# Experts on blocks of 96 places, with tokens held in the array in groups of 32 and four column groups of 256 weight columns

## The chip, the cores and the metric

The kernel runs on one core of a Trainium2 chip. The metric is device microseconds of one execution, taken as the median of several runs. Tensors are float32 throughout.

## What is computed

The program runs two hybrid transformer layers and then a third one of another kind; the change touches only the mixture of experts that ends the third. There are 1024 tokens of width 1024 (`D`), 32 experts in 4 groups of 8, and each token goes to the best two experts of its best group:

```python
logit_g = (h @ w_rg + b_rg).astype(F32)
grp = jnp.argmax(logit_g, axis=-1)
...
top_v, top_i = lax.top_k(logit_e, TOP_K)                    # TOP_K = 2
gate = jax.nn.softmax(top_v, axis=-1) * p_grp
expert = (grp[:, None] * EXPERTS_PER_GROUP + top_i).reshape(-1)
...
def expert_block(args):
    xb, e = args
    g, u = jnp.split(xb @ w_up[e], 2, axis=-1)              # w_up[e]: 1024 x 1024
    return (jax.nn.silu(g) * u) @ w_down[e]                 # w_down[e]: 512 x 1024
...
y = y[dest] * gate.reshape(-1)[order][:, None].astype(h.dtype)
return jax.ops.segment_sum(y, tok_sorted, num_segments=n_tok)
```

The 2048 pairs of token and expert are sorted by expert and padded to whole blocks of places, so that each block has one expert. The reference uses 128 places a block, but its result doesn't depend on that number. The reference's own routing, worked out on its inputs, gives the 32 experts between 43 and 87 tokens each, 2048 in all.

## The kernel before

Two functions matter. `mix_dispatch` (stage `disp`) scores the tokens, counts them per expert, and builds three tables: `rows` (which row of `XN` each place of each block takes), `gates` (the weight of each place) and `table` (the expert of each block, and the numbers of pairs of blocks). Its long chain of small VectorE steps ends at line 3245. While that runs, SyncE already loads the weights of the first block.

`block_experts` (stage `bexp`, lines 3384 to 3576) then runs over the blocks, two per turn of a hardware loop whose count is read from `table`; `i` is the turn and `j` the buffer, 0 or 1. Each engine has its own program with the same loop:

- SyncE loads the weights of block `n + 2` into the buffers of block `n`: the gate half and the up half of `w_up` (2 MB each, L3437, in rows of 2 KB), and `w_down` (2 MB in rows of 4 KB, L3439). Its order is gate, up, down for `j = 0`, then for `j = 1`. It waits for the last product that reads each buffer (`gate_done`, `up_done`, `downed`).
- TensorE, in `body`: eight products of 512 columns into `gu[0]` (the gate, L3537), the four transposes of the last block's middle values (`hid_turn`, L3515), eight products into `gu[1]` (the up half), eight transposes of the next block's tokens (`turn`, L3509), and the last block's second product (`down`, L3525, two halves of four products of 512 columns into `acc`). The tokens (`xT`, 128 by 128) are stationary, and the weights stream. So the order is up(n), down(n-1), up(n+1), down(n).
- ScalarE takes the exponential of the gate (L3492), copies the transposed middle values out of PSUM (`take`, L3480) and writes the result times the gate weight (`write`, L3486, two of 512 columns).
- VectorE finishes the silu and multiplies by the up half (L3564 to L3572), and then scales and shifts the next block's transposed tokens into `xT` (`modulate`, L3557).
- GpSimd multiplies by the layer's output gate (L3451), adds the block's rows to `F` with an indirect DMA (L3458), and gathers the rows of a block four further on with another (L3447).

After the last block, `gather_norm` reads `F`, normalises it and stores the result.

An fp32 product is two MATMUL records in the trace, each with its weight load (LDWEIGHTS, engine PEld); a transpose is one. The kernel already has one place where tokens in a group of 32 are held stationary and four column groups of 256 weight columns follow one another: the context part of `down` in the first layer's experts, line 2043 (stage `l0exp`).

Of the kernel before, what the change touches and what calls it, by code (L numbers as in the profile page):

```python
# [3042 lines left out]
MAX_BLOCKS = (SEQ * TOP + N_EXP * 127) // 128  # L3043
# [3 lines left out]
def mix_dispatch(nc, name, GO, wt, gt, X, cols_a, cols_b, w_group, b_group, w_expert, b_expert, consts, XN, F, rows, gates, table, w_up, w_down,  # L3047
# [6 lines left out]
    with Stage(nc, name) as st:  # L3054
# [10 lines left out]
        row_of = cst[:, 336:336 + T]  # L3065
        spare = cst[:, 336 + T:337 + T]
        places = cst[:, 337 + T:337 + T + 128]
# [27 lines left out]
        in_place = sb("in_place", [128, TOP * T, 128])  # L3095
# [9 lines left out]
        slot_sum = acc[1][:, 0:2 * MAX_BLOCKS]  # L3105
# [5 lines left out]
        steps, exps, counted, tabled = sem("steps"), sem("exps"), sem("counted"), sem("tabled")  # L3111
        marks = {}
        with nc.Block(no_gpsimd_drain=True) as block:
            @block.vector
            def _(ve):
# [81 lines left out]
                for q in range(1, SEQ // 128):  # L3197
                    step(V_.scalar_tensor_tensor(nb[:, :], cnt[:, 0:N_EXP], float(128 * q), nb[:, :], ALU.is_gt, ALU.add))
# [8 lines left out]
                step(V_.tensor_scalar(pstart[:, :], pstart[:, :], 128.0, None, ALU.mult))  # L3207
# [5 lines left out]
                step(V_.tensor_scalar(inside[:, :], flat, 1.0 / 128, 1.0, ALU.mult, ALU.subtract))  # L3213
# [3 lines left out]
                step(V_.scalar_tensor_tensor(at_place[:, :], inside[:, :], -128.0, flat, ALU.mult, ALU.add))  # L3217
# [3 lines left out]
                for half in range(2):  # L3221
                    part = slice(half * each, (half + 1) * each)
                    step(V_.tensor_tensor(in_place[:, part, :], places.unsqueeze(1).broadcast_to([128, each, 128]),
                                          at_place[:, part].unsqueeze(2).broadcast_to([128, each, 128]), ALU.is_equal))
# [10 lines left out]
                step(V_.tensor_scalar(rows[:, :], slot_sum[:, 0:MAX_BLOCKS], spare, None, ALU.add))  # L3235
                marks["rows"] = count[0]
                step(V_.tensor_copy(gates[:, :], slot_sum[:, MAX_BLOCKS:2 * MAX_BLOCKS]))
# [10 lines left out]
            def _(sp):  # L3248
# [23 lines left out]
                for h in range(2):  # L3272
                    sp.dma_start(first_w[h], w_up[bass.ds(e, 1), :, h * FF:(h + 1) * FF].rearrange("e (k p) n -> p (e k) n", p=128)).then_inc(first_in[h], 16)
                sp.dma_start(first_w[2], w_down[bass.ds(e, 1), :, :].rearrange("e (k p) n -> p (e k) n", p=128)).then_inc(first_in[2], 16)
# [3 lines left out]
            @block.gpsimd  # L3278
            def _(po):
                nc.gpsimd.memset(eps[:, :], EPS).then_inc(eps_made, 1)  # L3280
                for j in range(NX):
                    po.wait_ge(stored[j], START + 16 * (T // NX))
                po.wait_ge(steps, START + marks["rows"])
                for j in range(2):
                    po.indirect_dma_start(first_x[j], None, XN, bass.IndirectOffsetOnAxis(ap=rows[:, j:j + 1], axis=0)).then_inc(x_in[j], 16)

            @block.scalar
            def _(act):
# [32 lines left out]
                nc.scalar.activation(e1[:, :], e1[:, :], ACT.Exp).then_inc(exps, 1)  # L3321

# [61 lines left out]
def block_experts(nc, name, XN, rows, gates, F, out_gate, table, cols_a, cols_b, w_up, w_down, first_w, first_in, first_x, x_in, identity):  # L3384

    B = 2
    with Stage(nc, name, LOOPED) as st:
        sb, ps, sem = st.sb, st.ps, st.sem
        wu = [first_w[0:2], [sb(f"wu1{h}", [128, KD, FF]) for h in range(2)]]
        wd = [first_w[2], sb("wd1", [128, KF, D])]  # L3390
        og = sb("og", [128, D])
        idx = [sb(f"idx{j}", [128, 1], i32) for j in range(B)]
        out_idx = [sb(f"out_idx{j}", [128, 1], i32) for j in range(B)]
        xg = first_x
        xT = [sb(f"xT{j}", [128, KD, 128]) for j in range(B)]
        ex = sb("ex", [128, FF])
        hidR = [sb(f"hidR{j}", [128, FF]) for j in range(B)]
        hid = [sb(f"hid{j}", [128, KF, 128]) for j in range(B)]
        y = [sb(f"y{j}", [128, D]) for j in range(B)]
        turnedP = ps("turned", [128, KD, 128])  # L3400
        gu = [ps(f"gu{h}", [128, FF]) for h in range(2)]
        hidP = ps("hidP", [128, KF, 128])
        acc = [ps(f"acc{c}", [128, 512]) for c in range(2)]
        gate_in, up_in, down_in = ([st.adopt(first_in[i]), sem(f"{n}1")] for i, n in enumerate(("gate_in", "up_in", "down_in")))
        turned, x_ready, gate_done, up_done, hid_turned, hid_taken, downed, y_ready, freed, raised, steps = (
            [sem(f"{n}{j}") for j in range(B)] for n in ("turned", "x_ready", "gate_done", "up_done", "hid_turned", "hid_taken",
# [4 lines left out]
        passed_ve, passed_po, passed_act = sem("passed_ve"), sem("passed_po"), sem("passed_act")  # L3411

        def turns(eng, body):
            rest = eng.value_load(table[0:1, MAX_BLOCKS + 1:MAX_BLOCKS + 2], min_val=1, max_val=MAX_BLOCKS // 2 - 1)
            body(0, 0, True, False)
            with eng.Fori(0, rest) as i:
                body(i, 1, False, False)
                body(i + 1, 0, False, False)
            body(rest, 1, False, True)
            return rest  # L3420

        with nc.Block(no_gpsimd_drain=True) as block:
# [19 lines left out]
            def _(po):  # L3442
                def gather(i, j):
                    wait_alone(po, turned[j], LOOPED + i, passed_po)
                    nc.gpsimd.tensor_copy(idx[j][:, :], rows[:, bass.ds(i * B + j, 1)]).then_inc(idx_made[j], 1)
# [3 lines left out]
                def add_out(i, j, first):  # L3449
                    wait_alone(po, y_ready[j], LOOPED + i * 2 + 2, passed_po)  # L3450
# [4 lines left out]
                    nc.gpsimd.tensor_copy(out_idx[j][:, :], rows[:, bass.ds(i * B + j, 1)]).then_inc(out_made[j], 1)  # L3455
# [20 lines left out]
            def _(act):  # L3476
                def take(i, j):
                    act.wait_ge(hid_turned[j], LOOPED + i + 1)
                    act.wait_ge(downed[j], LOOPED + i * 2)
                    nc.scalar.activation(hid[j][:, :, :], hidP[:, :, :], ACT.Copy).then_inc(hid_taken[j], 1)  # L3480

                def write(i, j):
                    for c in range(2):
                        act.wait_ge(downed[j], LOOPED + i * 2 + c + 1)
                        wait_alone(act, freed[j], LOOPED + i, passed_act)
                        nc.scalar.activation(y[j][:, c * 512:(c + 1) * 512], acc[c][:, :], ACT.Copy, scale=gates[:, bass.ds(i * B + j, 1)]).then_inc(y_ready[j], 1)  # L3486

                def body(i, j, first, last):
                    act.wait_ge(gate_done[j], LOOPED + i + 1)
                    if not first:  # L3490
                        act.wait_ge(steps[1 - j], LOOPED + (i + j) * 4)
# [352 lines left out]
```

## Time and profile before

| | before |
|---|---|
| median of 3 runs | 4724.09 us (4721.94 to 4727.69) |
| the profiled execution, its span | 4732.4 us |
| instructions | 59744 |
| TensorE busy (matmul) | 4229.9 us (89%) |
| VectorE busy | 2033.2 us (43%) |
| ScalarE busy | 1069.4 us (23%) |
| GpSimd busy | 738.1 us (16%) |
| DMA traffic | 769.59 MB, mean 163 GB/s |
| weights of the last experts (L3437) | 64 issues of 2 MB, median 16.0 and 16.7 us to landing |

The profile is of one execution; its own time is the span of 4732.4 us, which is 8.3 us (0.18%) above the median of the runs, and no time around it is recorded. Busy shares are means over the whole program; a change in one stage is read from that stage. The stage of the last experts reaches from about 3979 us to 4704 us.

### The profile page before, as it was taken

What the parts mean: (1) busy time and instruction counts of PE and PEld (TensorE: products, weight loads), DVE (VectorE), ACT (ScalarE), POOL (GpSimd) and SP (SyncE); (2) the same over time, 40 slices, a digit from 0 to 9 for tenths busy, and PEclk for the clock granted to TensorE, in tenths of its full rate; (3) what the DMA queues carried; (4) which work ended last, traced back from release to release, by engine and by line L of the source; (5) the groups of instructions that cost most, each with busy time, mean ns of one, the idle gap of its engine ahead of it and who ended that gap; (6) DMA issues with size and microseconds to landing.
All of it is one profiled execution on the core that took longest, in us unless ns stands there. A gap on an engine that the chain in (4) does not pass through costs nothing. (4 is left out here: it accounts for less than half of the span.)

```text
span 4732.4 us, 59744 instructions
## 1 busy us (share of the span) xinstructions
PE 4229.9 (89%) x22975; PEld 2790.0 (59%) x22975; DVE 2033.2 (43%) x3879; ACT 1069.4 (23%) x2077; POOL 738.1 (16%) x851
## 2 busy tenths in 40 slices
PE   6998999977999798999968997999788896999996
PEld 4664556445888565566436885776566454444443
DVE  1223556135555322556254452111686666333332
ACT  1112346030000110335130001110564421111111
POOL 0110000301111011000301100000550330222221
PEclk8998999988999899999978998999899897999998
DMA  7115110367887411401169995111532115999997
GB/s 252 36 47 125 23 42 7 129 254 273 274 267 252 138 62 57 108 1 48 44 250 326 338 327 168 49 37 42 144 86 87 59 40 209 316 334 339 334 334 244
DMA packets 366851, 769.59 MB, mean 163 GB/s; under 512 B 59716, under 2 KB 136172, under 8 KB 365384
## 3 DMA queue, kind: packets, MB, share of 16 engines
q1 hardware_dynamic: 337032, 653.92, 40.2%
q0 software_dynamic: 23856, 90.19, 7.4%
q10 hardware_dynamic: 5712, 22.02, 1.2%
q8 instruction: 172, 2.82, 0.2%
q14 instruction: 79, 0.65, 0.0%
HBM read 650.62 MB, written 115.45 MB: 162 GB/s over the span
## 5 line engine op out<-in xcount | busy, mean ns | idle before, releaser
L3537 PE MATMUL bexp_gu<-X,bexp_xT 128*128 128x512 f32 x512 | 227.6, 598 | 3.0 <-DVE bexp_xT L3557 3.0
L3537 PE MATMUL bexp_gu<-bexp_wu,bexp_xT 128*128 128x512 f32 x512 | 225.1, 592 | 3.1 <-DVE bexp_xT L3557 3.1
L625 PE MATMUL p_ring<-p_hT,p_wc 128*128 128x256 f32 x1008 | 220.4, 381 | 4.8 <-DMA p_wc<-in_w_in 4.8
L625 PEld LDWEIGHTS p_ring<-p_hT,p_wc 128*128 128x128 f32 x1008 | 192.3, 191 | 31.6 <-issue 5.2
L3564 DVE TENSOR_SCALAR bexp_ex<-bexp_ex 128x512 f32<-128x512 f32 x32 | 15.1, 471 | 368.7 <-ACT bexp_ex L3492 368.7
L633 PE MATMUL p_ring<-p_wt,p_hT 128*128 128x400 f32 (+2 forms) x480 | 170.8, 516 | 0.0
L3537 PEld LDWEIGHTS bexp_gu<-X,bexp_xT 128*128 128x128 f32 x512 | 97.0, 192 | 119.8 <-issue 116.5
L3537 PEld LDWEIGHTS bexp_gu<-bexp_wu,bexp_xT 128*128 128x128 f32 x512 | 95.9, 190 | 117.7 <-issue 117.7
L1117 PE MATMUL l0mla_scores<-l0mla_kT,l0mla_qT 96*128 96x512 f32 (+1 forms) x312 | 142.9, 546 | 21.1 <-DMA l0mla_qT<-RT 15.3
L2026 PE MATMUL l0exp_gu<-l0exp_xT,l0exp_wg 128*128 128x160 f32 x1024 | 155.0, 305 | 4.5 <-DVE l0exp_xT L2070 4.5
L2026 PE MATMUL l0exp_gu<-l0exp_xT,l0exp_wu 128*128 128x160 f32 x1024 | 151.1, 301 | 1.5 <-DMA l0exp_wu<-in_exp_w_up 1.5
L2026 PEld LDWEIGHTS l0exp_gu<-l0exp_xT,l0exp_wg 128*128 128x128 f32 x1024 | 143.7, 192 | 11.4 <-issue 6.2
L3451 POOL TENSOR_TENSOR bexp_y<-bexp_y,bexp_og 128x1024 f32<-128x1024 f32 x32 | 75.0, 2344 | 481.6 <-ACT bexp_y L3486 481.6
L2043 PE MATMUL l0exp_acc<-l0exp_wd,l0exp_hid 128*32 128x256 f32 (+1 forms) x768 | 144.1, 455 | 2.6 <-DVE l0exp_hid L2085 2.6
L2026 PEld LDWEIGHTS l0exp_gu<-l0exp_xT,l0exp_wu 128*128 128x128 f32 x1024 | 144.0, 192 | 1.9 <-DMA l0exp_wu<-in_exp_w_up 1.9
L1117 PE MATMUL l1mla_scores<-l1mla_kT,l1mla_qT 96*128 96x512 f32 (+1 forms) x288 | 133.8, 551 | 12.3 <-DMA l1mla_qT<-RT 12.3
L3486 ACT ACTIVATE bexp_y<-bexp_acc,slot_gates 128x512 f32<-128x512 f32 x64 | 44.0, 687 | 419.6 <-PE bexp_acc L3525 419.6
L633 PEld LDWEIGHTS p_ring<-p_wt,p_hT 128*128 128x128 f32 x480 | 91.1, 190 | 76.1 <-issue 38.3
L2026 PE MATMUL l1exp_gu<-l1exp_xT,l1exp_wg 128*128 128x128 f32 x1024 | 127.4, 279 | 3.0 <-DMA l1exp_wg<-in_exp_w_gate 3.0
L2026 PEld LDWEIGHTS l1exp_gu<-l1exp_xT,l1exp_wg 128*128 128x128 f32 x1024 | 123.2, 195 | 10.6 <-issue 7.2
L2026 PE MATMUL l1exp_gu<-l1exp_xT,l1exp_wu 128*128 128x128 f32 x1024 | 125.7, 276 | 3.0 <-DMA l1exp_wu<-in_exp_w_up 3.0
L633 PE MATMUL l0proj_ring<-l0proj_wt,l0proj_hT 128*128 128x464 f32 x320 | 126.2, 552 | 0.0
(683 smaller groups left out, 8392.9 us busy)
## 6 DMA issues: line engine op xcount, KB each, us to landing
X<-in_w_expert_up SPq DMA_DIRECT2D x32, 2048.0 KB, 16.0
bexp_wu<-in_w_expert_up SPq DMA_DIRECT2D x32, 2048.0 KB, 16.7
l0exp_wg<-in_exp_w_gate SPq DMA_DIRECT2D x16, 2048.0 KB, 9.3
l0exp_wu<-in_exp_w_up SPq DMA_DIRECT2D x16, 2048.0 KB
l0exp_wd<-in_exp_w_down SPq DMA_DIRECT2D x16, 2048.0 KB, 12.6
l1exp_wg<-in_exp_w_gate SPq DMA_DIRECT2D x16, 2048.0 KB, 9.5
l1exp_wu<-in_exp_w_up SPq DMA_DIRECT2D x16, 2048.0 KB
l1exp_wd<-in_exp_w_down SPq DMA_DIRECT2D x16, 2048.0 KB, 13.1
```

What stands on the lines that cost most here:

```text
L625: mm = nc.tensor.matmul(out[:, i * PC:(i + 1) * PC], wc[:, k, b * 128:(b + 1) * 128], hT[ch % 2][:, k, :], start=(k == 0), stop=(k == KD - 1))
L633: mm = nc.tensor.matmul(out[:, at_out:at_out + n], hT[ch % 2][:, k, t * 128:(t + 1) * 128], wt[:, k, s:s + n], start=(k == 0), stop=(k == ...
L1117: mm = nc.tensor.matmul(scores[u % NBUF][:, at:at + n], qT[p % 2][a][:, row:row + 128], k[:, r:r + n], start=True, stop=True)
L2026: mm = nc.tensor.matmul(gu[g % 2][:, h, :], w[j][:, k, f * 128:(f + 1) * 128], xT[j][:, k, :], start=(k == 0), stop=(k == KD - 1))
L2043: mm = nc.tensor.matmul(acc[g % 3][cap * q:cap * (q + 1), 0:n_y], hid[j][:, f, at[s]:at[s] + cap], wd[j][:, f, at_y:at_y + n_y], start=(f ...
L3451: nc.gpsimd.tensor_tensor(y[j][:, :], y[j][:, :], og[:, :], ALU.mult).then_inc(weighed[j], 1)
L3486: nc.scalar.activation(y[j][:, c * 512:(c + 1) * 512], acc[c][:, :], ACT.Copy, scale=gates[:, bass.ds(i * B + j, 1)]).then_inc(y_ready[j], 1)
L3537: mm = nc.tensor.matmul(gu[h][:, :], xT[j][:, k, :], wu[j][h][:, k, :], start=(k == 0), stop=(k == KD - 1))
L3564: nc.vector.tensor_scalar(ex[:, :], ex[:, :], 1.0, None, ALU.add).then_inc(steps[j], 1)
```

## The change

A block has 96 places instead of 128, in three groups (`r`) of 32. In `block_experts` the stationary operand is now a group of 32 tokens, and four products (`c` = 0 to 3) with a quarter of the weight columns each go to the four column groups of the array, and so to the four 32-partition groups of PSUM. The up product of a group holds 128 gate columns and the matching 128 up columns in one bank, so that gate and up are no longer two phases; the three groups are. The middle values lie with their quarter `c` on a partition group, so three transposes of 128 by 128 give the stationary operands of `down`. `w_up` of a block is one load of 4 MB with rows of 4 KB. The result is written by ScalarE in twelve pieces of 32 by 256. In `mix_dispatch` the tables are made for 96 places; ScalarE makes the copies of the gate weights on four partition groups. The loop of ScalarE, VectorE and TensorE opens with a wait for SyncE (`opened`). The core of the diff:

```diff
-MAX_BLOCKS = (SEQ * TOP + N_EXP * 127) // 128
+BLOCK = 96
+GROUPS = BLOCK // 32
+MAX_BLOCKS = (SEQ * TOP + N_EXP * (BLOCK - 1)) // BLOCK
 MAX_BLOCKS += MAX_BLOCKS % 2
...
-                for q in range(1, SEQ // 128):
-                    step(V_.scalar_tensor_tensor(nb[:, :], cnt[:, 0:N_EXP], float(128 * q), nb[:, :], ALU.is_gt, ALU.add))
+                for q in range(1, -(-SEQ // BLOCK)):
+                    step(V_.scalar_tensor_tensor(nb[:, :], cnt[:, 0:N_EXP], float(BLOCK * q), nb[:, :], ALU.is_gt, ALU.add))
...
-                step(V_.tensor_copy(gates[:, :], slot_sum[:, MAX_BLOCKS:2 * MAX_BLOCKS]))
...
+                act.wait_ge(steps, START + marks["rows"])
+                for c in range(4):
+                    for r in range(GROUPS):
+                        nc.scalar.activation(gates[32 * c:32 * c + 32, r, :], slot_sum[32 * r:32 * r + 32, MAX_BLOCKS:2 * MAX_BLOCKS], ACT.Copy).then_inc(gated4, 1)
+                act.wait_ge(gated4, START + 4 * GROUPS)
...
+    R = GROUPS
+    COLS = 4
+    HN = FF // COLS
+    YN = D // COLS
...
-        gu = [ps(f"gu{h}", [128, FF]) for h in range(2)]
-        acc = [ps(f"acc{c}", [128, 512]) for c in range(2)]
+        gu = [ps(f"gu{r}", [128, 512]) for r in range(R)]
+        acc = ps("acc", [128, 2, 2, YN])
...
         def turns(eng, body):
+            eng.wait_ge(opened, 1)
...
-                        for h, (done, landed) in enumerate(((gate_done, gate_in), (up_done, up_in))):
-                            sp.wait_ge(done[j], LOOPED + i)
-                            sp.dma_start(wu[j][h][:, :, :], w_up[bass.ds(e, 1), :, h * FF:(h + 1) * FF].rearrange("e (k p) n -> p (e k) n", p=128)).then_inc(landed[j], 16)
-                        sp.wait_ge(downed[j], LOOPED + i * 2)
+                        sp.wait_ge(up_done[j], LOOPED + i * R)
+                        sp.dma_start(wu[j][:, :, :], w_up[bass.ds(e, 1), :, :].rearrange("e (k p) n -> p (e k) n", p=128)).then_inc(up_in[j], 16)
+                        sp.wait_ge(downed[j], LOOPED + i * R)
...
                 def write(i, j):
-                    for c in range(2):
-                        act.wait_ge(downed[j], LOOPED + i * 2 + c + 1)
-                        wait_alone(act, freed[j], LOOPED + i, passed_act)
-                        nc.scalar.activation(y[j][:, c * 512:(c + 1) * 512], acc[c][:, :], ACT.Copy, scale=gates[:, bass.ds(i * B + j, 1)]).then_inc(y_ready[j], 1)
+                    wait_alone(act, freed[j], LOOPED + i, passed_act)
+                    for r in range(R):
+                        if r != 0:
+                            act.wait_ge(downed[j], LOOPED + i * R + r + 1)
+                        if r == 0:
+                            act.wait_ge(downed[j], LOOPED + i * R + min(R, 2))
+                        for c in range(COLS):
+                            rows_c = slice(32 * c, 32 * c + 32)
+                            nc.scalar.activation(y[j][32 * r:32 * r + 32, c * YN:(c + 1) * YN], acc[rows_c, r // 2, r % 2, :], ACT.Copy,
+                                                 scale=gates[rows_c, r, bass.ds(i * B + j, 1)]).then_inc(y_ready[j], 1)
...
-                    for c in range(2):
+                    for r in range(R):
                         for f in range(KF):
-                            mm = nc.tensor.matmul(acc[c][:, :], hid[j][:, f, :], wd[j][:, f, c * 512:(c + 1) * 512], start=(f == 0), stop=(f == KF - 1))
+                            for c in range(COLS):
+                                mm = nc.tensor.matmul(acc[32 * c:32 * c + 32, r // 2, r % 2, :], hid[j][:, r, 32 * f:32 * f + 32],
+                                                      wd[j][:, f, c * YN:(c + 1) * YN], start=(f == 0), stop=(f == KF - 1))
                         mm.then_inc(downed[j], 1)
...
-                    for h in range(2):
-                        pe.wait_ge((gate_in, up_in)[h][j], LOOPED + (i + 1) * 16)
+                    pe.wait_ge(up_in[j], LOOPED + (i + 1) * 16)
+                    for r in range(R):
+                        if not first:
+                            pe.wait_ge(steps[1 - j], LOOPED + (i + j) * 4 * R - 4 * (R - 1 - r))
                         for k in range(KD):
-                            mm = nc.tensor.matmul(gu[h][:, :], xT[j][:, k, :], wu[j][h][:, k, :], start=(k == 0), stop=(k == KD - 1))
-                        mm.then_inc((gate_done, up_done)[h][j], 1)
-                        if h == 0 and not first:
+                            both = wu[j][:, k, :].rearrange("p (h c n) -> p h c n", h=2, c=COLS)
+                            for c in range(COLS):
+                                mm = nc.tensor.matmul(gu[r][32 * c:32 * c + 32, 0:2 * HN].rearrange("p (h n) -> p h n", h=2), xT[j][:, k, 32 * r:32 * r + 32],
+                                                      both[:, :, c, :], start=(k == 0), stop=(k == KD - 1))
+                        mm.then_inc(up_done[j], 1)
+                        if r == 0 and not first:
                             hid_turn(i + j - 1, 1 - j)
```

VectorE's four silu steps run three times on 128 by 128 instead of once on 128 by 512. GpSimd's gather and its indirect add handle 96 rows a block, and its multiplication waits for all twelve pieces.

## Rows read from the trace of the kernel before

**Rows 1.** The page's second part, DMA share in tenths, 40 equal slices.
```profile
DMA  7115110367887411401169995111532115999997
```

**Rows 2.** Busy time by stretch: PE, PEld, DVE, ACT, POOL, granted clock, DMA share, GB/s.
```profile
4050.00:4200.00 150.00, 150.00 (x413) 70.85 (x412) 54.85 (x84) 16.49 (x28) 37.03 (x35) 1.00 0.98 335
```

**Rows 3.** Timeline of TensorE over one block: start, length, engine, line, tile, records.
```profile
4115.06 7.03 PE L3537 MATMUL bexp_gu<-X,bexp_xT 128*128 128x512 f32 x16
4121.92 0.60 PE L3515 MATMUL bexp_hidP<-identity,bexp_hidR 128*128 128x128 f32 x4
4122.36 7.03 PE L3537 MATMUL bexp_gu<-X,bexp_xT 128*128 128x512 f32 x16
4129.23 1.04 PE L3509 MATMUL bexp_turned<-identity,X 128*128 128x128 f32 x8
4130.10 7.03 PE L3525 MATMUL bexp_acc<-bexp_wd,bexp_hid 128*128 128x512 f32 x16
4136.97 7.03 PE L3537 MATMUL bexp_gu<-bexp_wu,bexp_xT 128*128 128x512 f32 x16
```

**Rows 4.** Timeline of SyncE over the same block: the issues of weight loads.
```profile
4115.39 0.37 SPq L3439 DMA_DIRECT2D YA<-in_w_expert_down  x1
4116.59 3.14 SPq L3437 DMA_DIRECT2D bexp_wu<-in_w_expert_up  x2
4137.30 0.37 SPq L3439 DMA_DIRECT2D bexp_wd<-in_w_expert_down  x1
```

**Rows 5.** DMA queues, 4050 to 4650 us: packets, MB, share of 16 engines.
```profile
q1 hardware_dynamic: 71214, 172.52, 80.2%
q0 software_dynamic: 7776, 28.32, 17.7%
```

**Rows 6.** Busy time by stretch, for the DMA share and GB/s that end each row.
```profile
4115.30:4118.00 2.70, 2.70 (x7) 1.14 (x6) 0.00 (x0) 0.69 (x1) 1.74 (x1) 1.00 0.61 124
4124.80:4130.20 5.40, 5.40 (x20) 2.82 (x19) 3.33 (x3) 0.00 (x0) 0.00 (x0) 1.00 1.04 297
4131.00:4137.00 6.00, 6.00 (x16) 2.65 (x15) 2.17 (x7) 0.69 (x1) 0.00 (x0) 1.00 1.04 391
11.50:31.50 20.00, 11.12 (x120) 4.30 (x124) 0.00 (x0) 1.69 (x5) 0.22 (x1) 0.91 1.03 423
```

**Rows 7.** Line 2043: timeline of TensorE, its last 32 records as a stretch, weight loads.
```profile
1506.65 8.89 PE L2043 MATMUL l0exp_acc<-l0exp_wd,l0exp_hid 128*128 128x512 f32 x48
1515.48 2.44 PE L2026 MATMUL l0exp_gu<-l0exp_xT,l0exp_wg 128*128 128x160 f32 x16
...
1513.60:1515.35 1.75, 1.75 (x33) 0.94 (x32) 1.00 0.97 359
...
L2043 PEld LDWEIGHTS l0exp_acc<-l0exp_wd,l0exp_hid 128*32 128x32 f32 x512 | 15.0, 109 | 20.4 <-issue 12.1
```

**Rows 8.** Timeline of TensorE: a long run of records on column groups of 32.
```profile
3803.34 2.22 PE L2704 MATMUL gs_bank<-gs_v,gs_kbT 128*32 128x64 f32 x144
3805.48 0.70 PE L2649 MATMUL gs_acc<-out_wt,NT 128*128 128x512 f32 x1
```

**Rows 9.** Groups by line and form: busy us and mean ns.
```profile
L2081 DVE RECIPROCAL l1exp_ex<-l1exp_ex 128x128 f32<-128x128 f32 x64 | 61.0, 954 | 2.2
L2380 ACT ACTIVATE da_probT<-da_turned 128x256 f32<-128x256 f32 x32 | 12.0, 375 | 3.3 <-PE da_turned L2326 3.3
L3557 DVE TENSOR_SCALAR bexp_xT<-bexp_turned,cols 128x128 f32<-128x128 f32 x256 | 84.5, 402 | 9.5 <-PE bexp_turned L3509 4.7 <-issue 3.0
```

**Rows 10.** The stage's start: timelines of TensorE and SyncE, and a stretch.
```profile
3979.81 1.96 PE L3509 MATMUL bexp_turned<-identity,X 128*128 128x128 f32 x8 [6.21 <-DMA X<-XN,slot_rows]
3980.72 0.34 SPq L3426 DMA_DIRECT2D bexp_og<-gates  x1
4001.20:4005.40 4.20, 1.06 (x10) 0.82 (x8) 3.33 (x9) 0.00 (x0) 1.15 (x2) 1.00 1.04 387
```

**Rows 11.** DMA queues, 2520 to 2870 us, where TensorE's code has no loop.
```profile
q8 instruction: 19, 0.31, 0.4%
```

More of the change, by code:

```diff
@@ L3104, in mix_dispatch @@
         cnt = acc[0][:, 512:1024]
-        slot_sum = acc[1][:, 0:2 * MAX_BLOCKS]
+        slot_sum = acc[1][0:BLOCK, 0:2 * MAX_BLOCKS]
         w_in, eps_made = sem("w_in"), sem("eps_made")
@@ L3405, in block_experts @@
-        turned, x_ready, gate_done, up_done, hid_turned, hid_taken, downed, y_ready, freed, raised, steps = (
-            [sem(f"{n}{j}") for j in range(B)] for n in ("turned", "x_ready", "gate_done", "up_done", "hid_turned", "hid_taken",
+        wu = [first_w[0], sb("wu1", [128, KD, 2 * FF])]
+        wd = [first_w[1], sb("wd1", [128, KF, D])]
+        og = sb("og", [BLOCK, D])
+        idx = [sb(f"idx{j}", [BLOCK, 1], i32) for j in range(B)]
+        out_idx = [sb(f"out_idx{j}", [BLOCK, 1], i32) for j in range(B)]
@@ L3407, in block_experts @@
+        up_in, down_in = ([st.adopt(first_in[i]), sem(f"{n}1")] for i, n in enumerate(("up_in", "down_in")))
+        turned, x_ready, up_done, hid_turned, hid_taken, downed, y_ready, freed, raised, steps = (
+            [sem(f"{n}{j}") for j in range(B)] for n in ("turned", "x_ready", "up_done", "hid_turned", "hid_taken",
                                                          "downed", "y_ready", "freed", "raised", "steps"))
@@ new lines, in body @@
+                def body(i, j, first, last):
+                    for r in range(R):
+                        act.wait_ge(up_done[j], LOOPED + i * R + r + 1)
+                        if not first:
+                            act.wait_ge(steps[1 - j], LOOPED + (i + j) * 4 * R - 4 * (R - 1 - r))
+                        nc.scalar.activation(ex[r][:, :], gu[r][:, 0:HN], ACT.Exp, scale=-1.0).then_inc(raised[j], 1)
+                        if r == 0 and not first:
+                            take(i + j - 1, 1 - j)
@@ L3490, in body @@
                     if not first:
-                        act.wait_ge(steps[1 - j], LOOPED + (i + j) * 4)
-                    nc.scalar.activation(ex[:, :], gu[0][:, :], ACT.Exp, scale=-1.0).then_inc(raised[j], 1)
-                    if not first:
-                        take(i + j - 1, 1 - j)
                         write(i + j - 1, 1 - j)
@@ L3764, in second_block @@
         table = keep("table", [128, MAX_BLOCKS + 3], i32)
-        rows, block_gates = keep("slot_rows", [128, MAX_BLOCKS], i32), keep("slot_gates", [128, MAX_BLOCKS])
+        rows, block_gates = keep("slot_rows", [128, MAX_BLOCKS], i32), keep("slot_gates", [128, GROUPS, MAX_BLOCKS])
         YA = keep("YA", [128, LAT_TILES, A_HEADS * A_DV])
-        first_x = [X[:, j, :] for j in range(2)]
-        half = KD * FF // D
-        first_w = [X[:, CTX_TILES + h * half:CTX_TILES + (h + 1) * half, :].rearrange("p a n -> p (a n)").rearrange("p (k n) -> p k n", n=FF) for h in range(2)]
+        first_x = [X[0:BLOCK, j, :] for j in range(2)]
+        first_w = [X[:, CTX_TILES:CTX_TILES + KD, :]]
         first_w.append(YA[:, :, :].rearrange("p a n -> p (a n)").rearrange("p (k n) -> p k n", n=D))
-        first_in = [nc.alloc_semaphore(f"first_{n}_in") for n in ("gate", "up", "down")]
+        first_in = [nc.alloc_semaphore(f"first_{n}_in") for n in ("up", "down")]
         x_in = [nc.alloc_semaphore(f"first_x_in{j}") for j in range(2)]
```

111 lines of the change are left out of this document (54 added, 57 removed).

## The prediction

> **What bounds the kernel now.** I read the page's 40 slices first: the last experts fill the slices near 9 at the end of the DMA row [rows 1]. Then the busy time of a stretch inside that stage: TensorE is busy 150.00 of 150 us at the full clock (1.00, the 2.4 GHz level), the 16 DMA engines 98%, at 335 GB/s; VectorE, ScalarE and GpSimd 55, 16 and 37 us [rows 2]. So two resources are nearly full, and the question is which binds. The timeline of TensorE answers it: one block is gate 6.87 us (start to start), middle transposes 0.44, up 6.87, token transposes 0.87, down 6.87, and the next block starts at once; 4136.97 − 4115.06 = 21.91 us, with no gap [rows 3]. The timeline of SyncE shows how near the DMA is: all 6 MB of a bunch (down weights of block n, up weights of block n+1) are issued when down(n) ends, 4115.39 to 4116.59, and the next bunch at 4137.30 [rows 4]. A bunch has one block period to arrive. It nearly fills it: 80.2% of 21.91 us is weights (17.6 us), 17.7% gather and indirect add (3.88 us) [rows 5]. Of the period 2.7 us is a start at 124 GB/s, which moves what 391 GB/s moves in 0.86: 1.84 us are lost between issue and full rate [rows 6]. TensorE binds, the DMA follows at under 1 us.
>
> **The change, part by part.** *Number of blocks.* The reference's routing gives an expert at most 87 tokens, under 96, so 32 blocks stay 32, and weight traffic stays 6.29 MB a block.
>
> *TensorE's products.* Before: 24 products of 512 columns, two records each, 6.87/16 = 0.429 us a record, 20.6 us a block [rows 3]. After: up has 3 groups × 8 × 4 products, down 3 × 4 × 4, 144 products, 288 records of 256 columns. One alone should take half of 0.429; what matters is whether four column groups run side by side. Line 2043 has this very form: 128 rows, 32 stationary columns, 256 moving. From its start to the next line's are 8.83 us; 16 records of 512 columns take 6.87, which leaves 1.96 for 32 records, and the stretch of these 32 alone has 1.75 [rows 7]. So four records (a "four") take 1.75/8 = 0.219 us, as long as one: the overlap is full, and 0.21 us goes to entering and leaving the form. A burst of 32 might live off a filled queue; but 144 records on groups of 32 run in 2.14 us, 14.9 ns each, where I need one per 55 ns, so issue doesn't limit a long run [rows 8]. Per block: 72 fours × 0.219 = 15.8; token transposes 0.87; three of four middle transposes 0.33; two runs between transposes at 0.21, 0.42. P = 17.4 us (from 17.0 without the changes of form to 18.9 if each four costs 1.96/8). This moves work off the path: up 10.5 us, down 5.3.
>
> *Other engines, hidden.* VectorE has three chains on 128 columns; the last group's is a reciprocal of 0.95, three steps and an exponential of under 0.4 each, then `modulate`'s eight at 0.33 busy (84.5/256) [rows 9]: about 5.4 us after the up products end, and TensorE first does transposes and down, 0.87 + 5.3 = 6.2. It hides with 0.8 us left; without that cover each further microsecond would be one per block. ScalarE's twelve pieces at about 0.375 [rows 9] are 4.5 us; the first eight start a group before down ends, the rest end 2.5 us after it, ahead of the next exponential, 3.5 us into the next up. Behind them waits GpSimd (all twelve), 2 us later than before; its gather is for a block more than a period away. ScalarE's waits on `downed` queue only that exponential.
>
> *Weights.* The 4 MB load is one piece: up can't start on its first half, so a bunch must land whole by the start of the block two after. SyncE still issues at the end of down; its wait for `up_done` had always passed by then [rows 4]. Transfer time S: 6.29 MB at 391 GB/s (2 KB rows) is 16.1 us, at 423 (4 KB rows, the load of the program's start, no other traffic) 14.9 [rows 6]; all rows are 4 KB now, but gathers run beside: I take 15.7. Gather and add fall by a quarter, 3.88 to 2.9; while they run both together move only 297 GB/s [rows 6]. S = 18.6 (17.8 to 19.0; by the share of busy time, 17.6 + 2.9 = 20.5).
>
> *The sum of a period.* With P = 17.4 TensorE no longer binds. From the end of down(n): 1.84 us of start, S, then up(n+3) may begin, and P later down(n+2) ends: two periods = 1.84 + 18.6 + 17.4 = 37.8, 18.9 each. That is above S and P, so it sets the pace. Gain 21.91 − 18.9 = 3.0 us a block.
>
> *The ends.* At the start stand three more small steps of VectorE's `nb` chain, and the wait for `opened`, behind which TensorE now loads the count: its first transposes, at 3979.81 before, can't come ahead of SyncE's opening, which ends just before its first issue at 3980.72 [rows 10]. For both I take 2 us late (0 to 3, an estimate from these two starts), but block 0's up is 3 us shorter, so block 1 starts where it did. Blocks 1 and 2 gain 4.5 each; block 3 waits 3.0 for the first bunch: −6. Blocks 3 to 30: 28 × 3.0 = −84. The last block and its down gain 6.6 and lose 2.0 to the late pieces: −4.6. Sum −95: from the median 4724 to 4629, and the span from 4732 to about 4638; the profiled execution stands 0.18% above the median, and I carry the difference over.
>
> **A rule and the rows.** The Trainium skill (TensorE: Matmul & The Clock Gate, Part 3: Packing small matmuls — row/col tiling) measured 3.07 times for four row groups and 2.38 for three column groups. By 3.07 a four would take 4 × 0.215/3.07 = 0.28 us, an estimate, and P 21.8: no gain at all. The rows above show 0.219, a factor of 3.9, and I go by them.
>
> **The rivals.** *Weights bind harder.* If the start is lost on every bunch (1.84 + 18.6 = 20.4) or S is the busy share's 20.5, a period is 20.5: 28 × 1.4 = 39, and 8 at the ends: 4677. For it: the share is measured in this very loop. Against: it counts packets as busy while they wait at the start of a bunch, and a bunch issued while another flows has no start. The two don't add: for the kernel before they would make 17.6 + 3.9 + 1.84 = 23.3, more than the 21.91 measured. With a fetch of code on top (next) it could reach 4710.
>
> *Code.* The loop's TensorE code grows from 60 to 299 records a block. No instruction traffic stands in the loop before [rows 5], while straight code fetches 19 packets of 16 KB in 350 us [rows 11]. If each turn must fetch again at its jump, it costs about what a load's start costs, 1.8 to 2.7 us per two blocks [rows 6], partly inside the wait for weights: at most 15 × 2.7 = 40, 4669. The Trainium skill (Runtime: NRT & Kernel Launch, Instruction fetch mechanics) says both that TensorE's code memory has 128 KiB, in which this loop fits, and that only two blocks of 16 KiB are held and a jump out of them stalls; no run here shows which.
>
> *The fours don't hold up.* The up products read their 256 columns in two runs of 128, over 48 fours, which no row shows. The point of no change is 0.282 us a four ((21.9 − 1.6)/72). If one weight load per four were exposed (109 ns each; they now overlap, 15.0 us busy for 512 [rows 7]), a four is 0.33, P = 25.3, and 31 × 3.4 − 5 makes 4824. Idle TensorE could also lose its clock; but after 3.1 idle us of 4.2 it was still 1.00 [rows 10].
>
> *More blocks.* If the chip's routing pushed an expert over 96, the loop would take two more blocks: 4629 + 38 = 4667. Nothing but a rounding at a margin of nine tokens speaks for it.
>
> **How the numbers follow.** Weights and TensorE in turn at 18.2 to 19.8 a block: 0.55, 4607 to 4656. Weights harder or code fetched again, 4660 to 4712: 0.26. Fours slower: 0.10, of which 0.02 near no change. More blocks 0.03. Unnamed stalls 0.06, in thirds to a half. Low end: S 17.8 and P 17.0 give 18.3, 17 less, and 5 at the ends: 4606. The high end reaches to 4700, over most of the harder weights, and leaves out the slow rival and a few more, under 2 in 10. A measurement of this kernel tells 0.2% (9 us) from no change. Faster 0.85 (0.55 + 0.24 + 0.03 + 0.03), same 0.05, slower 0.10.
>
> **What would show it.** In the profile after: fours 0.22 us apart at the new up and down lines; TensorE idle some 1.5 us a block before the first up product, ended by the load of `w_up`; periods alternating near 17.4 to 20.4 or even at S; DMA share 0.98 or more at 370 to 390 GB/s; 32 indirect adds; no instruction queue in the loop. It would be wrong if VectorE's `modulate` ended the wait before up (its 0.8 us gone), if fours stood at 0.28 or more, or if the clock in the stage fell under 1.00.

## The result and the profile after

The median went from 4723.0 to 4697.6 us, a ratio of 0.9936 with a 95% interval of 0.9924 to 0.9949: 25 us faster where the prediction had 95. The profiled execution took 4688.9 us; its span, 4687.0, is 45.4 less than that of before, and 13.5 of these lie in unchanged code ahead of the stage. The first matmul of the count in `mix_dispatch`, before and after (timelines of TensorE):

```profile
3953.00 1.22 PE L3374 MATMUL disp_acc<-disp_both,disp_cst 128*128 128x256 f32 x2 [13.20 <-DVE disp_upto L3186]
...
3939.47 1.22 PE L3380 MATMUL disp_acc<-disp_both,disp_cst 128*128 128x256 f32 x2 [13.21 <-DVE disp_upto L3189]
```

From there to the end are 779.4 us before and 747.5 after, so the stage itself gave 31.9 us, and that is the number to explain. TensorE is no longer busy all the time, and its granted clock is under full, 0.95 (busy time by stretch, columns as in [rows 2]):

```profile
4050.00:4200.00 150.00, 129.00 (x2153) 74.38 (x2149) 62.85 (x146) 53.60 (x124) 37.56 (x36) 0.95 0.93 336
```

Blocks now come in pairs of unlike length. Timeline of TensorE over one pair, columns as in [rows 3]; the bracket is the idle time ahead and what ended it:

```profile
4116.39 5.35 PE L3561 MATMUL bexp_gu<-bexp_wu,bexp_xT 128*32 128x256 f32 x64 [5.16 <-DMA bexp_wu<-in_w_expert_up]
4121.67 0.55 PE L3535 MATMUL bexp_hidP<-identity,bexp_hidR 128*128 128x128 f32 x3
4122.15 7.11 PE L3561 MATMUL bexp_gu<-bexp_wu,bexp_xT 128*32 128x256 f32 x128
4129.19 0.88 PE L3529 MATMUL bexp_turned<-identity,X 96*128 96x96 f32 x8
4130.00 5.39 PE L3546 MATMUL bexp_acc<-YA,bexp_hid 128*32 128x256 f32 x96
4135.21 3.64 PE L3561 MATMUL bexp_gu<-X,bexp_xT 128*32 128x256 f32 x64
4138.78 0.55 PE L3535 MATMUL bexp_hidP<-identity,bexp_hidR 128*128 128x128 f32 x3
...
4158.07 5.06 PE L3561 MATMUL bexp_gu<-bexp_wu,bexp_xT 128*32 128x256 f32 x64 [5.57 <-DMA bexp_wu<-in_w_expert_up]
```

The products are as fast as hoped: 64 records (16 fours) in 4138.78 − 4135.21 = 3.57 us, 0.223 a four; the down product's 24 fours in 5.21 us, 0.217. But from block 3 to block 29 every odd block waits over 5 us for `bexp_wu`. Behind the first of the two waits shown, the first 64 records take 5.28 us instead of 3.57: in that stretch the granted clock is 0.68, between the two levels of 1.2 and 2.4 GHz (0.50 and 1.00), so part of it ran at the lower one. The pair lasts 41.68 us, 18.82 and 22.86. The timeline of SyncE shows when its loads were issued:

```profile
4111.43 0.37 SPq L3451 DMA_DIRECT2D bexp_wd<-in_w_expert_down  x1
4113.00 0.38 SPq L3449 DMA_DIRECT2D X<-in_w_expert_up  x1
4135.59 0.37 SPq L3451 DMA_DIRECT2D YA<-in_w_expert_down  x1
4136.81 0.37 SPq L3449 DMA_DIRECT2D bexp_wu<-in_w_expert_up  x1
4152.69 0.37 SPq L3451 DMA_DIRECT2D bexp_wd<-in_w_expert_down  x1
```

The bunch of 4135.59 (call it A) meets a DMA that has run dry; the bunch of 4152.69 (B) is issued while A still flows. Busy time by stretch, for the last three columns (clock, DMA share, GB/s): the time around A's first issue, A's start, a stretch after it, the time of the bunch B before A, and the slow 64 records:

```profile
4135.20:4136.50 1.30, 1.30 (x28) 0.78 (x24) 0.00 (x0) 1.23 (x4) 0.00 (x0) 1.00 0.00 0
4136.50:4139.20 2.70, 2.70 (x47) 1.48 (x39) 0.00 (x0) 2.57 (x6) 0.00 (x0) 1.00 0.90 247
4139.20:4144.00 4.80, 4.80 (x90) 2.89 (x92) 3.44 (x3) 1.42 (x5) 3.29 (x3) 1.00 1.02 416
...
4116.00:4134.00 18.00, 17.61 (x279) 10.33 (x283) 7.10 (x19) 1.49 (x5) 4.86 (x5) 0.91 1.02 378
4116.40:4121.70 5.30, 5.30 (x65) 2.83 (x65) 0.00 (x0) 0.00 (x0) 3.67 (x5) 0.68 1.03 423
```

Blocks 3 and 31 and the end of the stage, timeline of TensorE and then of ScalarE:

```profile
4032.42 1.93 PE L3561 MATMUL bexp_gu<-bexp_wu,bexp_xT 128*32 128x256 f32 x16 [6.21 <-DMA bexp_wu<-in_w_expert_up]
...
4613.58 5.35 PE L3561 MATMUL bexp_gu<-bexp_wu,bexp_xT 128*32 128x256 f32 x64 [3.48 <-DMA bexp_wu<-in_w_expert_up]
...
4636.59 8.15 PE L3546 MATMUL bexp_acc<-bexp_wd,bexp_hid 128*32 128x256 f32 x96 [4.48 <-ACT bexp_hid L3492]
...
4630.07 5.87 ACT L3503 ACTIVATE bexp_y<-bexp_acc,slot_gates 32x256 f32<-32x256 f32 x12 [3.20 <-PE bexp_acc L3546]
4635.97 0.49 ACT L3492 ACTIVATE bexp_hid<-bexp_hidP 128x384 f32<-128x384 f32 x1
```

The last block's middle tile stands on ScalarE behind the twelve pieces of the block before. TensorE waits 4.48 us for it and then takes 8.15 us for a down product of 5.2.

### The profile page after: what moved, and what is told of

It reads as the page before. It is cut to its first block and busy times, and to the rows that moved or that the text cites. A ratio compares the mean times of both kernels' runs of the same rounds, so it can differ in the third digit from the quotient of the medians.

```text
span 4687.0 us, 76558 instructions
## 1 busy us (share of the span) xinstructions
PE 4100.3 (87%) x30623; PEld 2786.7 (59%) x30623; DVE 2057.6 (44%) x4137; ACT 1213.1 (26%) x2473; POOL 734.7 (16%) x851
## 5 line engine op out<-in xcount | busy, mean ns | idle before, releaser
L3561 PE MATMUL bexp_gu<-bexp_wu,bexp_xT 128*32 128x256 f32 x3072 | 202.9, 428 | 82.9 <-DMA bexp_wu<-in_w_expert_up 78.4
L3503 ACT ACTIVATE bexp_y<-bexp_acc,slot_gates 32x256 f32<-32x256 f32 x384 | 179.1, 466 | 144.4 <-PE bexp_acc L3546 135.6
L625 PEld LDWEIGHTS p_ring<-p_hT,p_wc 128*128 128x128 f32 x1008 | 192.3, 191 | 31.7 <-issue 5.3
L3561 PEld LDWEIGHTS bexp_gu<-bexp_wu,bexp_xT 128*32 128x32 f32 x3072 | 107.3, 123 | 173.2 <-issue 124.9
L3590 DVE TENSOR_SCALAR bexp_ex<-bexp_ex 128x128 f32<-128x128 f32 x96 | 52.4, 546 | 336.0 <-ACT bexp_ex L3511 336.0
L3561 PE MATMUL bexp_gu<-X,bexp_xT 128*32 128x256 f32 x3072 | 174.1, 383 | 2.7 <-DVE bexp_xT L3582 2.7
L3463 POOL TENSOR_TENSOR bexp_y<-bexp_y,bexp_og 96x1024 f32<-96x1024 f32 x32 | 75.7, 2364 | 457.5 <-ACT bexp_y L3503 457.5
L3561 PEld LDWEIGHTS bexp_gu<-X,bexp_xT 128*32 128x32 f32 x3072 | 98.3, 111 | 70.8 <-issue 5.0
L1995 ACT ACTIVATE l0exp_ex<-l0exp_gu 128x160 f32<-128x160 f32 x64 | 19.5, 304 | 444.4 <-PE l0exp_gu L2026 444.4
## 6 DMA issues: line engine op xcount, KB each, us to landing
X<-in_w_expert_up SPq DMA_DIRECT2D x16, 4096.0 KB, 21.9
```

Of the source, the lines that this page charges most:

```text
L625: mm = nc.tensor.matmul(out[:, i * PC:(i + 1) * PC], wc[:, k, b * 128:(b + 1) * 128], hT[ch % 2][:, k, :], start=(k == 0), stop=(k == KD - 1))
L1995: nc.scalar.activation(ex[g % 2][:, :], gu[g % 2][:, 0, :], ACT.Exp, scale=-1.0).then_inc(raised, 1)
L3463: nc.gpsimd.tensor_tensor(y[j][:, :], y[j][:, :], og[:, :], ALU.mult).then_inc(weighed[j], 1)
L3503: nc.scalar.activation(y[j][32 * r:32 * r + 32, c * YN:(c + 1) * YN], acc[rows_c, r // 2, r % 2, :], ACT.Copy, scale=gates[rows_c, r, bass ...
L3561: mm = nc.tensor.matmul(gu[r][32 * c:32 * c + 32, 0:2 * HN].rearrange("p (h n) -> p h n", h=2), xT[j][:, k, 32 * r:32 * r + 32], both[:, : ...
L3590: nc.vector.tensor_scalar(ex[r][:, :], ex[r][:, :], 1.0, None, ALU.add).then_inc(steps[j], 1)
```

## The experiments

The theory after these readings: TensorE's part of the prediction holds, and what was lost is lost because SyncE issues a load late; the DMA then starts from a standstill, TensorE waits, and its clock falls. "Stage" in the table is from block 0's first up product to the end of the span; "a block" is the time from block 8's start to block 30's, by 22. Both are of the profiled execution. The kernels were timed on several occasions, so each median goes with the before beside it.

| kernel | median, us | before beside it | ratio (95%) | stage | a block |
|---|---|---|---|---|---|
| before | 4723.0 | | | 747.7 | 21.91 |
| after | 4697.6 | 4723.0 | 0.9936 (0.9924 to 0.9949) | 715.0 | 20.80 |
| e1_order | 4616.2 | 4726.7 | 0.9764 (0.9748 to 0.9780) | 635.9 | 18.45 |
| e2_warm | 4684.2 | 4726.7 | 0.9909 (0.9892 to 0.9925) | 705.4 | 20.25 |
| e3_eighth | 4590.4 | 4726.7 | 0.9713 (0.9693 to 0.9732) | 603.4 | 17.10 |
| e4_order_before | 4723.9 | 4726.7 | 0.9997 (0.9987 to 1.0006) | 747.8 | 21.91 |
| e5_tail | 4608.2 | 4721.6 | 0.9761 (0.9743 to 0.9779) | 630.1 | 18.51 |
| e6_half_rows | 4583.5 | 4721.6 | 0.9703 (0.9683 to 0.9722) | 601.9 | 17.10 |
| e7_halves | 4625.7 | 4721.6 | 0.9788 (0.9771 to 0.9804) | 643.8 | 18.73 |
| e8_skip | 4607.8 | 4728.8 | 0.9745 (0.9729 to 0.9761) | 626.9 | 18.38 |

**The order of the loads.** In the pair above the up product that reads `bexp_wu` ends at 4129.19, and its next load is issued at 4136.81, because the wait for `downed` of the block before stands in front of it. Each up load moves ahead of that wait. In outline, not in the words of the kernel (the loop's last turn leaves out the load that has no block):

```diff
-    up_done[j]  -> load wu[j] of block n;    downed[j] -> load wd[j] of block n
+    up_done[1]  -> load wu[1] of block 2i+1; downed[0] -> load wd[0] of block 2i
+    up_done[0]  -> load wu[0] of block 2i+2; downed[1] -> load wd[1] of block 2i+1
```

> The changed kernel with one thing moved: SyncE issues the up weights of the next block as soon as up_done frees their buffer, ahead of the down weights that wait for downed. Same bytes, same instructions on TensorE. Theory (the late issue sets the pace): the transfers then run back to back at the 18.0 us that the second bunch of a pair took, so a block takes 18.2 to 18.6 us in place of 20.7 to 20.8, the wait for bexp_wu falls from 5.2 to 6.2 us to under 1 us, the granted clock of 4050 to 4500 us rises from 0.94 to at least 0.98, and 28 blocks give 60 to 70 us: 4628 to 4640 us. Rival (the DMA engines are full: 94% of 20.7 us is 19.5 us of packet time a block, whoever issues them): a block takes 19.5 to 20.7 us, TensorE keeps waiting, 4663 to 4698 us.

Measured: 81 us less than the changed kernel by the medians, 79 in the stage. In its loop the clock and the DMA are at full, and the waits are 1.0 to 1.8 us where under 1 was expected (a stretch; the first and the last block that the table's 18.45 is counted from):

```profile
4050.00:4200.00 150.00, 143.64 (x2504) 84.42 (x2500) 76.71 (x171) 59.05 (x138) 41.22 (x40) 1.00 1.03 380
...
4124.53 1.72 PE L3573 MATMUL bexp_gu<-X,bexp_xT 128*32 128x256 f32 x28 [1.84 <-DMA X<-in_w_expert_up]
...
4530.41 3.66 PE L3573 MATMUL bexp_gu<-X,bexp_xT 128*32 128x256 f32 x64 [1.05 <-DMA X<-in_w_expert_up]
```

The theory stands, and the rival that the DMA engines were full at 94% falls: they moved the same bytes in 18.45 us a block. The gain is above the 60 to 70 expected mainly because blocks 2 to 6 run at TensorE's own 17.10 us, their loads being ahead; only from block 7 on do the transfers bind.

**The same order in the kernel before.** The edit is the same, with its two up loads.

> The kernel before with the same move of SyncE's loads (up weights of the next block ahead of the down weights). Theory (TensorE sets its pace, no wait for weights in its loop): within 0.2% of 4723 us. Rival (the order of the loads is worth something by itself): 20 us or more faster.

Measured 2.8 us less, inside the interval of no change. The order is worth nothing while TensorE takes 21.9 us; it is the change that makes it matter.

**TensorE alone.** The loads in the loop shrink to one tile each, and the rest of the products reads what the buffers held (the same for `wd`):

```diff
-    sp.dma_start(wu[j][:, :, :], w_up[bass.ds(e, 1), :, :] ...)
+    sp.dma_start(wu[j][:, 0:1, :], w_up[bass.ds(e, 1), 0:128, :] ...)
```

> The changed kernel with only the first of the eight (up) and four (down) weight tiles loaded in the loop, 0.5 MB each instead of 4.2 and 2.1 MB; the rest of the products reads what the buffers held, so this part of the computation is left out. Theory (TensorE's own work is what the prediction said, and all beyond it is the loads): no wait for weights, granted clock 1.00, a block takes TensorE's 17.1 to 17.5 us, 28 blocks save 90 to 103 us: 4595 to 4610 us. Rival (something else in the block's chain, GpSimd's gather or ScalarE's twelve pieces, stands close behind): 18.5 us or more a block, 4635 us or more.

```profile
4050.00:4200.00 150.00, 150.00 (x2627) 89.06 (x2623) 83.10 (x176) 61.03 (x143) 43.50 (x42) 1.00 0.44 110
```

17.10 us a block, each one the same, TensorE never idle. Nothing but the loads stands between the changed kernel and TensorE's pace; with the DMA less than half busy, neither ScalarE's pieces nor VectorE nor the gather is next in line.

**The clock by itself.** TensorE's wait is filled with work and the loads are left as they were:

```diff
+    if j == 1 and not last:
+        for _ in range(24):
+            nc.tensor.matmul(hidP[:, 3, :], identity[:, :], identity[:, :], start=True, stop=True)
     pe.wait_ge(up_in[j], LOOPED + (i + 1) * 16)
```

> The changed kernel with 24 matmuls of the identity by itself put on TensorE ahead of its wait for the up weights in every odd body of the loop (some 5 us of work, into a part of hidP that nothing reads): the wait of 5.2 to 6.2 us is filled, the loads are untouched. Theory (the lower granted clock after the wait is a cost of its own): the first 64 matmuls of the up product take 3.6 us again in place of 5.3 to 6.4, and as the end of the block's down product issues the next bunch, what is won goes into the pair's 41.5 us until the other bunch, which has 1.3 us to spare, binds: 1.2 to 2 us a pair, 15 to 28 us in all, 4670 to 4683 us. Rival (the loads alone set the pace, TensorE's speed after the wait is given back at the next wait): within 0.2% of the changed kernel, 4690 to 4705 us.

```profile
4158.62 5.39 PE L3546 MATMUL bexp_acc<-bexp_wd,bexp_hid 128*32 128x256 f32 x96
4163.94 5.62 PE L3556 MATMUL bexp_hidP<-identity 128*128 128x128 f32 x48
4169.50 3.66 PE L3564 MATMUL bexp_gu<-bexp_wu,bexp_xT 128*32 128x256 f32 x64
...
4186.62 3.64 PE L3564 MATMUL bexp_gu<-X,bexp_xT 128*32 128x256 f32 x64
...
4050.00:4200.00 150.00, 146.91 (x2404) 92.80 (x2407) 64.57 (x151) 49.46 (x116) 36.91 (x36) 1.00 0.97 344
```

The up product takes 3.59 us again and the granted clock is 1.00. A block falls from 20.80 to 20.25 us, 15 us over 28 blocks. Block 1, which had no wait for weights to fill, starts 7 us later after block 0 than without the filling (25.1 against 18.1 us), so the stage won 9.6 and the median 13, just under the 15 to 28 expected and outside the rival's range. The lower clock is a cost of its own; the rest of what was lost is the load's.

**The tail.** On top of e1_order, VectorE makes half of the pieces of the last two blocks:

```diff
-    write(i + j - 1, 1 - j)                 # ScalarE, last body
+    write(i + j - 1, 1 - j, range(0, 2))    # ScalarE: columns 0 to 511
+    write(i + j - 1, 1 - j)                 # VectorE: columns 512 to 1023
```

> e1_order with one more thing changed, in the last body only: of the twelve pieces of each of the last two blocks VectorE makes six (columns 512 to 1023), ScalarE the other six. In e1_order ScalarE takes the last middle tile only behind all twelve pieces of the block before, and TensorE waits 4.47 us for that; the last twelve pieces take 5.86 us. Theory (ScalarE's small pieces made the tail longer than predicted): the wait falls by 2.5 to 3 us and the last pieces by 2.5 to 3 us, so from the last up product to the end 65 to 67 us in place of 71.4, that is 4.5 to 6 us less than e1_order. Rival (VectorE's pieces take as long beside GpSimd's multiplication, or the two engines hinder each other in the same banks): less than 1.5 us.

Timelines of e5_tail, then the last down product of e1_order, and the two last down products as stretches, e1_order first (the granted clock is the third number from the end):

```profile
4543.30 3.64 PE L3573 MATMUL bexp_gu<-bexp_wu,bexp_xT 128*32 128x256 f32 x64
...
4561.64 5.39 PE L3558 MATMUL bexp_acc<-bexp_wd,bexp_hid 128*32 128x256 f32 x96 [1.53 <-ACT bexp_hid L3504]
...
4565.46 2.92 ACT L3515 ACTIVATE bexp_y<-bexp_acc,slot_gates 32x256 f32<-32x256 f32 x6 [3.95 <-PE bexp_acc L3558]
...
4568.83 8.22 PE L3558 MATMUL bexp_acc<-bexp_wd,bexp_hid 128*32 128x256 f32 x96 [4.47 <-ACT bexp_hid L3504]
...
4569.00:4578.00 9.00, 8.05 (x96) 3.70 (x92) 0.00 (x0) 2.38 (x6) 3.30 (x3) 0.69 0.30 44
4561.60:4567.00 5.40, 5.36 (x96) 3.13 (x96) 1.36 (x3) 1.46 (x4) 3.82 (x3) 1.00 0.16 12
```

From the last up product to the end 62.9 us (4606.2 − 4543.30) in place of 71.4 in e1_order: 8.5 less, where 4.5 to 6 were expected. The wait gave 2.9 and the last pieces 2.9, as expected; the other 2.8 is the down product, 5.39 instead of 8.22: after 1.53 us of idle time its granted clock is 1.00, after e1_order's 4.47 it is 0.69. At 4608 us this beats both kernels, as e1_order does. By the ratios to the before beside them the two runs are alike (0.9761 and 0.9764), so the 8.5 us rest on the two profiles.

**What the transfers consist of.** e1_order is bound by 18.45 us of transfers a block, and the prediction had put 2.9 of 18.6 on gather and adding. By the packets' own time that was right. The DMA view of e1_order from 4200 to 4500 us (packets, MB, share):

```profile
q1 hardware_dynamic: 25594, 102.67, 86.0%
q0 software_dynamic: 3584, 12.58, 16.9%
```

Of 18.45 us these shares are 15.9 for the weights and 3.1 for gather and adding; together they are 3% over, since packets overlap. Three runs ask what a block wins when a part goes. First, half of the rows left out (`idx[j][0:BLOCK // 2, :]`, and so for the adding):

> e1_order with the gather of tokens and the adding of outputs cut to 48 of the 96 rows; half of the places are left out of the computation. In e1_order a block takes 18.4 to 18.5 us with the DMA engines never idle. Theory (the prediction's sum of a bunch: weights 15.7 us and gather with adding 2.9 us, each in proportion to its bytes): 18.45 less 1.45 is 17.0 us, so TensorE's 17.1 us binds: 17.1 to 17.2 us a block, 24 blocks save 30 to 32 us of e1_order. Rival (an indirect transfer costs by the transfer and not by the row, or the weights alone take 18 us): 18.0 us or more a block, under 12 us saved.

17.10 us a block: TensorE binds. A block's up weights land 15.9 us after their issue (the DMA view's median) instead of 25.4. So 48 rows are worth at least 1.35 us; how much more is hidden by TensorE. Second, in e5_tail the empty places are skipped, which read and wrote a spare row before (their row numbers now lie beyond the tensor):

```diff
-    bass.IndirectOffsetOnAxis(ap=idx[j][:, :], axis=0))
+    bass.IndirectOffsetOnAxis(ap=idx[j][:, :], axis=0), bounds_check=ROWS - 1, oob_is_err=False)
```

> e5_tail with the empty places taken out of the indirect transfers: a place without a token gets a row number beyond the tensor, and gather and adding skip it (before, it read and wrote a spare row). 2048 of the 32 x 96 = 3072 places hold a token, so a third of the rows goes. Nothing of the result is left out. Theory (the gather and the adding, an estimated 2.9 us of the 18.45, go by rows moved): 18.45 less 0.95 is 17.5 us a block, 24 blocks save 20 to 25 us of e5_tail: 4582 to 4590 us, TensorE waiting under 0.5 us for its weights. Rival (a skipped row costs its place in the queue all the same): within 0.2% of e5_tail, 4600 to 4617 us.

The DMA view of 4200 to 4500 us, e5_tail's indirect queue and then e8_skip's (packets, MB, share):

```profile
q0 software_dynamic: 3584, 12.58, 16.9%
...
q0 software_dynamic: 3584, 8.41, 11.3%
```

A third of the bytes goes, and with it a third of the queue's packet time (5.6% of 18.45 us is 1.0 us a block), but not one packet. A block falls by 0.13 us only, not by 0.95; e1_order and e5_tail, whose loops are the same, differ by 0.06. So the theory that a block falls with what gather and adding move falls. It isn't that a skipped row keeps its cost: it leaves a packet of a few bytes, and beside the indirect transfers the DMA is no longer full. The DMA view of 4200 to 4500 us, e5_tail and then e8_skip, and a stretch of the indirect transfers of each (last two columns: DMA share, GB/s):

```profile
DMA packets 29083, 114.93 MB, mean 383 GB/s; under 512 B 1024, under 2 KB 1024, under 8 KB 29083
DMA packets 29405, 112.02 MB, mean 373 GB/s; under 512 B 2060, under 2 KB 2060, under 8 KB 29405
...
4278.00:4283.50 5.50, 5.50 (x100) 3.53 (x100) 4.11 (x12) 1.16 (x3) 0.00 (x0) 1.00 1.04 312
4246.50:4251.00 4.50, 4.50 (x80) 2.74 (x76) 2.92 (x9) 0.28 (x1) 0.00 (x0) 1.00 0.86 245
```

The two indirect stretches after that of e8_skip have shares of 0.97 and 0.92. Counted from the trace's packet records, at least 16 packets are in flight at every moment of these 300 us in e5_tail; in e8_skip there are fewer during 13% of them, always at the indirect transfers. So some of the 16 DMA engines stand idle while others are still at work, and TensorE goes on waiting for its weights (141.7 of 150 us busy from 4200 to 4350 us). Rows that lie on some engines more than on others would explain it, but the traces don't name a packet's engine, so this isn't shown. Third, the up weights in two loads with rows of 2 KB:

> e1_order with the up weights of an expert loaded in two halves of columns again (rows of 2 KB, 2.1 MB each) as in the kernel before, in place of one load with rows of 4 KB; TensorE waits for both. Same bytes. Theory (the transfer goes by bytes): a block stays at 18.4 to 18.5 us, within 0.2% of e1_order. Rival (longer rows move faster, and the change's single load was worth something): 18.8 us or more a block, 10 us or more slower than e1_order.

18.73 us a block instead of 18.45, and 8 us in the stage (643.8 against 635.9); the medians stand 9.5 apart, though the before beside this run was 5 us faster. That is between the two expectations: the change's single load with rows of 4 KB was worth some 1.5% of a block. Whether the rows or the number of loads did it, this run doesn't tell.

## Why the prediction was right in sign and wrong in size

The measured 4697.6 us stand at the upper end of the predicted range, which was opened that far for weights that bind harder, not for what happened.

**TensorE's products: right.** P was put at 17.4 us; e3_eighth shows 17.10, and fours of 0.217 to 0.223 where 0.219 stood. The rival that fours don't hold up is out. By the factor 3.07 that the Trainium skill (TensorE: Matmul & The Clock Gate, Part 3: Packing small matmuls — row/col tiling) has for four row groups, they would have been 0.28 us, an estimate. The trace disagrees for these column groups: 4 × 0.215/0.220 is 3.9, where 0.215 is half of a 512-column record's 0.429 in [rows 3].

**Weight transfer S: right.** 18.6 was predicted for a bunch; back to back it is 18.45. Its split agrees with the packets' shares, 15.9 and 3.1 us where 15.7 and 2.9 stood, and half of the rows was worth at least 1.35 us (e6_half_rows). What failed later, in e8_skip, was only the step from the bytes moved to the time of a block.

**The period: right in form, two terms too small.** The chain was the predicted one, from the end of down over start and bunch to the next up, and over TensorE's block to the next issue. But of the pair's predicted 37.8 us (1.84 + 18.6 + 17.4) each half grew. The first is 22.86 instead of 20.44: from the end of down to 4139.2, 4.0 us, only 2.7 × 247 GB/s arrive, which 416 GB/s moves in 1.6, so 2.4 are lost where 1.84 stood. The window of [rows 6] began only with the issue, in a kernel whose DMA was still at full rate in the last microsecond of the down product (before, busy time by stretch):

```profile
4114.00:4115.00 1.00, 1.00 (x3) 0.38 (x2) 0.00 (x0) 0.00 (x0) 0.00 (x0) 1.00 1.06 389
```

Here it stands at 0 GB/s for 1.3 us. The rest, with S at 18.45, is 2.0 us; B's packets, which flow among A's last, and the time from the last packet to the matmul belong to it, and I have not split them. The second half is 18.82 instead of 17.4. Its first 64 records run partly at the lower clock level; that was the prediction's own condition for being wrong. It argued from 3.1 idle microseconds in a stretch whose clock was still 1.00 [rows 10]; here they are over 5. Over blocks 3 to 31 a block takes (4613.58 − 4032.42)/28 = 20.76 us where 18.9 was predicted: 32 us won instead of 84. Of the 52 that are missing e2_warm gives back 15 and e1_order, which takes away the standstill and with it the idle time, all.

So the step that failed is this sum, in two of its terms: the start and transfer behind the late issue took 22.86 us where 20.44 stood, and TensorE's block behind the wait took 18.82 where 17.4 stood, at a full clock that it didn't have. e1_order shows that both go with the late issue. The prediction had seen it, in the remark that SyncE's wait for `up_done` had "always passed by then", and had it in the sum at too low a price; but a wait that has long passed when its turn comes says that the load could have been issued earlier, and I read it as harmless. Of the signs named ahead, the wait for `w_up` and the alternating periods came; the DMA share is 0.93 at 336 GB/s instead of 0.98 at 370 to 390, and the clock is under 1.00.

**The ends.** The opening costs 0.8 us (from the count's first matmul to block 0's up product 31.7 before, 32.5 after), not 2, but blocks 0 to 3 gave only 4.1 (64.6 to 60.4), so the start is −3.3 instead of −6: block 3 waits 6.2 us for the first bunch where 3.0 stood. The last up product to the end went from 69.5 to 73.4, +3.9 instead of −4.6. There the term of the late pieces was mis-sized twice: a piece takes 5.87/12 = 0.49 us, not 0.375, and I counted them behind the last product only, not ahead of the middle tile for which TensorE waits 4.48 us. The lower clock, put at nothing, adds 8.15 − 5.2 = 2.9 us in the last down product and 5.35 − 3.64 = 1.7 in the first records of the last up product. The sum is −32.5 − 3.3 + 3.9 = −31.9.

**The rivals.** Weights that bind harder gave 4677 for a period of 20.5 us. The period came near, 20.76, but not by that mechanism: only every second bunch starts from standstill, and the share of busy time, 94%, was no bound, as e1_order shows. Code fetched again is out. The DMA queues of the changed kernel from 4050 to 4600 us list no instruction packets, which [rows 11] has where code is fetched:

```profile
q1 hardware_dynamic: 41247, 165.53, 79.0%
q0 software_dynamic: 5824, 20.45, 15.1%
```

The Trainium skill (Runtime: NRT & Kernel Launch, Instruction fetch mechanics) has it both ways, 128 KiB for TensorE's code and two lines of 16 KiB. This loop, with about 1,200 matmuls and weight loads a turn, agrees with the 128 KiB. Blocks stayed 32. VectorE's `modulate` ended a wait of TensorE only ahead of blocks 0 and 1.

## What to carry to other kernels

When a change makes the bound engine faster, look at the issue order of the resource that is next: list for each load when its buffer comes free and when it is issued, and price the difference, even where it costs nothing now. In this loop a load into an idle DMA and a TensorE that waits cost more than the transfer's own time, so a period made of "start + transfer + compute" should be shortened by issuing earlier before any term in it is tuned. And small pieces that are hidden in a loop are counted again in its last turn, ahead of everything that stands behind them in the queue.

## What the runs showed of the hardware

- Skipped rows of an indirect transfer keep their packets, but not their time: 3584 packets in 300 us with and without the skipping, 8.41 MB instead of 12.58, a share of 11.3% instead of 16.9%. A block bound by transfers still took 18.38 us instead of 18.51, with fewer than 16 packets in flight during 13% of the time.
- A wait of TensorE of 5.16 us was followed by 5.30 us at a mean granted clock of 0.68; waits of 1.0 to 1.8 us in e1_order left it at 1.00.
- The same weights in two loads with rows of 2 KB instead of one with rows of 4 KB made a transfer-bound block 1.5% longer (18.73 against 18.45 us).
- VectorE's first step of a chain (L3590) took 2.20 us beside GpSimd's multiplication, against 0.23 to 0.30 for the same step of the two groups after it:

```profile
4139.89 2.38 POOL L3463 TENSOR_TENSOR bexp_y<-bexp_y,bexp_og 96x1024 f32<-96x1024 f32 x1 [17.40 <-ACT bexp_y L3503]
4140.16 2.20 DVE L3590 TENSOR_SCALAR bexp_ex<-bexp_ex 128x128 f32<-128x128 f32 x1 [5.62 <-ACT bexp_ex L3511]
...
4146.86 0.23 DVE L3590 TENSOR_SCALAR bexp_ex<-bexp_ex 128x128 f32<-128x128 f32 x1 [0.15 <-ACT bexp_ex L3511]
```
